# Down panels of the MLPs cut as 512, 272, 272 or 448, 448, 160 columns in place of three times 352

## What is computed

```python
hn = rmsnorm(x, p['norm_ffn_pre'][l])
f = jnp.square(jax.nn.relu(hn @ p['mlp_up'][l])) @ p['mlp_down'][l]
x = x + rmsnorm(f, p['norm_ffn_post'][l])
```

## Time and profile before

| | |
|---|---|
| time, two runs | 2158.47 and 2158.26 us, median 2158.36 |
| profiled execution, span from first to last instruction | 2155.1 us (its time with what lies around the span is not listed apart) |
| median of the runs less that span | 3.3 us |
| PE, PEld busy | 2146.0, 2135.0 us |
| DVE, ACT, POOL busy | 908.0, 652.9, 100.1 us |
| matmuls | 13496, of 352 columns but for the small products named above |
| the first of the four changed groups | its down units are evacuated from 591.30 to 679.02 us |

### The profile page before, as it was taken

How to read it: one execution, slowest core, us unless ns; L and a number is a source line. 1 busy time by engine, 2 the same in 40 slices (tenths; PEclk the granted TensorE clock), 3 DMA queues, 4 the chain that set the end, 5 groups by cost and what they waited for, 6 DMA issues and landing times.

```text
span 2155.1 us, 31488 instructions
## 1 busy us (share of the span) xinstructions
PE 2146.0 (100%) x13496; PEld 2135.0 (99%) x13496; DVE 908.0 (42%) x1414; ACT 652.9 (30%) x1105; POOL 100.1 (5%) x127
## 2 busy tenths in 40 slices
PE   9999999999999999999999999999999999999998
PEld 9999999999999999999999999999999999999998
DVE  8766367323322322334953333493223223322336
ACT  6673355202301310333511112453013103202332
POOL 2000000000000000000043231000000000000000
PEclk9999999999999999999999999999999999999999
DMA  5111422111111111141311114222111111111142
GB/s 165 35 41 40 139 88 72 50 40 49 50 42 47 49 50 40 49 135 44 120 50 47 43 50 139 67 84 59 42 48 50 49 40 50 50 42 48 50 140 81
DMA packets 208410, 138.65 MB, mean 64 GB/s; under 512 B 6000, under 2 KB 204784, under 8 KB 208272
## 3 DMA queue, kind: packets, MB, share of 16 engines
q1 hardware_dynamic: 207552, 135.51, 20.6%
q10 hardware_dynamic: 720, 1.13, 0.1%
HBM read 119.22 MB, written 17.40 MB: 63 GB/s over the span
## 4 chain that ended last, share of the span: by engine, by line
PE 99%; ACT 1%; DMA 0%; DVE 0%; issue 0%; DVEq 0%; ACTq 0%
PE ps L698 32%; PE ps L700 32%; PE ps L699 32%; PE ps L773 1%; PE ps L801 0%; PE ps L729 0%; PE ps L720 0%; DMA w_all_raw<-in_w_in_even_dram 0%; PE ps L716 0%; PE ps L784 0%; PE ps L760 0%; ACT L1074 0%; ACT L1030 0%; ACT lru L1030 0%; ACT lru L1032 0%; ACT gelu L1074 0%
## 5 line engine op out<-in xcount | busy, mean ns | idle before, releaser
L698 PE MATMUL ps<-x_hi,w_all 128*128 128x352 f32 x2304 | 747.0, 324 | 0.0
L700 PE MATMUL ps<-x_hi,w_all 128*128 128x352 f32 x2304 | 739.1, 321 | 0.0
L699 PE MATMUL ps<-x_lo,w_all 128*128 128x352 f32 x2304 | 739.1, 321 | 0.0
L698 PE MATMUL ps<-h_hi,w_all 128*128 128x352 f32 x1728 | 556.2, 322 | 0.0
L700 PE MATMUL ps<-h_hi,w_all 128*128 128x352 f32 x1728 | 555.2, 321 | 0.0
L699 PE MATMUL ps<-h_lo,w_all 128*128 128x352 f32 x1728 | 555.2, 321 | 0.0
L698 PEld LDWEIGHTS ps<-x_hi,w_all 128*128 128x128 f32 x2304 | 432.4, 188 | 2.7
L699 PEld LDWEIGHTS ps<-x_lo,w_all 128*128 128x128 f32 x2304 | 432.4, 188 | 2.2
L700 PEld LDWEIGHTS ps<-x_hi,w_all 128*128 128x128 f32 x2304 | 432.3, 188 | 0.0
L876 ACT CAST w_all<-w_all_raw 128x1024 fp32r<-128x1024 f32 x166 | 173.5, 1045 | 525.1 <-DMA w_all_raw<-in_mlp_down_dram 324.8
L698 PEld LDWEIGHTS ps<-h_hi,w_all 128*128 128x128 f32 x1728 | 324.5, 188 | 0.3 <-DVE h_lo L1452 0.3
(11 more groups left out here) (201 smaller groups left out, 1416.0 us busy)
## 6 DMA issues: line engine op xcount, KB each, us to landing
w_all_raw<-in_mlp_up_dram SPq DMA_DIRECT2D x60, 512.0 KB, 3.9
w_all_raw<-in_mlp_down_dram SPq DMA_DIRECT2D x60, 512.0 KB, 3.8
x_save<-f SPq DMA_DIRECT2D x9, 1408.0 KB, 6.0
x_old<-x_save SPq DMA_DIRECT2D x9, 1408.0 KB, 11.5
w_all_raw<-in_c_w_in_dram SPq DMA_DIRECT2D x22, 512.0 KB, 3.7
w_all_raw<-in_w_in_even_dram SPq DMA_DIRECT2D x12, 512.0 KB, 3.6
x_old<-in_x_cols_dram SPq DMA_DIRECT2D x3, 1408.0 KB, 12.8
w_all_raw<-in_w_out_even_dram SPq DMA_DIRECT2D x6, 512.0 KB, 3.8
```

Of the source, the lines that this page charges most:

```text
L698: nc.tensor.matmul(dst, wh, hi, start=(i == 0), stop=False)
L699: nc.tensor.matmul(dst, wh, lo, start=False, stop=False)
L700: last = nc.tensor.matmul(dst, wl, hi, start=False, stop=(i == KC - 1))
```

## The change

In the kinds `dn` with m other than 0 (4 groups of 7 panels, 28) the three units of a panel no longer take columns 0 to 352, 352 to 704 and 704 to 1056. With an odd m they take 512, 272 and 272, with an even m 448, 448 and 160. A table `columns` holds the bounds for each unit. PE reads h and VectorE updates f by that table (`cut`). The number of units, their order, their banks and all that surrounds them stay. The wait of an evacuation that adds to f is now for the last unit of the same panel number in the group before, since its pieces need not match. There are 12 panels with 160 columns and 16 with 272.

```diff
@@ -175,6 +175,9 @@
+    CUTS = ((0, 448, 896, TOK), (0, 512, 784, TOK))
+    columns = [(u.t * TT, (u.t + 1) * TT) if u.kind != "dn" or u.m == 0 else CUTS[u.m % 2][u.t:u.t + 2] for u in UNITS]
@@ -342,7 +345,11 @@
         def bank(n):
-            return ps[:, n % NB, 0:TT]
+            return ps[:, n % NB, 0:columns[n][1] - columns[n][0]]
+
+        def cut(buf, c, n):
+            c0 = c * (buf.shape[1] // KC)
+            return buf[:, c0 + columns[n][0]:c0 + columns[n][1]]
@@ -693,7 +700,7 @@
-                    hi, lo = pt(src[0], k, t), pt(src[1], k, t)
+                    hi, lo = [pt(b, k, t) if X else cut(b, k, n) for b in src]
@@ -1288,8 +1295,8 @@
                 if u.kind in ("dn", "dn3"):
-                    dve.wait_ge(evac_d, evac_no[n - 48] + 1)
-                    ins = nc.vector.tensor_tensor(pt(f, m, t), bank(n), pt(f, m, t), ALU.add)
+                    dve.wait_ge(evac_d, evac_no[n - 48 + NT - 1 - t] + 1)
+                    ins = nc.vector.tensor_tensor(cut(f, m, n), bank(n), cut(f, m, n), ALU.add)
```

## The result

The changed kernel takes **2192.7 us** (2192.46 to 2192.95, 2 runs) against 2158.36 (2158.26 to 2158.47, 2 runs): a ratio of 1.0159, 95% interval 1.0129 to 1.0188. It is 34.3 us slower where I forecast 10.2, and outside my range. The two profiled spans stand 35.4 us apart.

What follows compares the result with a forecast made beforehand. TensorE was taken as the bound: the number of matmuls times the distance at which they follow each other. The narrow piece's 10.2 us plus 0 for the rest, on 2158.4, gave 2168.6 us; range 2157 to 2180.

Steps and rivals of the forecast that it cites:

- Step 2: 160-column matmuls in even panels: each costs 35.5 ns more than a linear sum allows, x 288 = 10.2 us.
- floor: Least distance between matmuls that each bring a full set of weights: 0.111 us, hidden by 352 and 272 columns.
- the line: Linear cost of a matmul by its columns: 75.5 ns taken for 160, between 72.2 and 78.7.
- Step 1: Matmul count and columns in the cut panels: three pieces together cost the same, 476.7 ns; wider pieces cost nothing net.
- the 12 ns: Excess of a 352-column matmul's 158.9 ns over 146.7 at full clock, read as a fixed share or in proportion.
- Step 3: Where pieces begin: 3.84 or 3.80 us units differ in starting column; taken as zero, ends -1.0 and +1.9 us.
- Steps 4 to 6: VectorE's evacuations and subtractions, weight loads and casts, and the later down units' new wait: all covered, at no cost.
- A: Rival for the narrow matmuls: weight loads can follow closer than 0.111 us, so the change costs 0, 2158.4 us; 6%.
- B: Rival: narrow matmuls in the even panels fall to the full f32 rate, 267 ns each, 2213.6 us; 14%.
- C: Rival: half rate for the narrow piece, 145.3 ns each, 20.1 us more, 2178.5 us; 4%.
- D: Rival: the weight path sets 158.9 ns, so 272 and 160 columns cost that too; 36.9 us more, 2195.3 us; 5%.
- E: Rival: the granted clock drops in the thinner stretches, slower by over 2%; 1%.

Runs made afterwards that it cites:

- Experiment 9: The change with all 28 panels cut 512, 272, 272 and no narrower piece; 2162.13 us against 2157.79 for the kernel before, ratio 1.002.
- experiments 4 and 7: One extra 272-column matmul ahead of each of four up groups: in the kernel before (4), 2178.76 us against 2158.42; in the changed kernel (7), 2172.55 against 2157.79.
- experiment 8: The changed kernel with twelve other cuts in m = 1 to 6 and m = 7 back to 352 columns; 2177.39 us against 2158.76.

## Why the prediction was wrong

*Step 2, the narrow piece: right.* I said 111 ns for a floor and 75.5 for the line, 10.2 us. Measured: 111.7, and the line through 272 (125.1) and 512 (232.5) gives 75.0 at 160. 36.7 x 288 = 10.6 us. The row that carried it was the distance of two weight loads behind matmuls that take no time. The trace after has the loads of the narrow unit at the same distance:

```profile
621.92 0.19 PEld L706 LDWEIGHTS ps<-h_lo,w_all 128*128 128x128 f32 x1
622.03 0.19 PEld L707 LDWEIGHTS ps<-h_hi,w_all 128*128 128x128 f32 x1
622.14 0.19 PEld L705 LDWEIGHTS ps<-h_hi,w_all 128*128 128x128 f32 x1
```

*Step 1, "the three pieces together cost the same": mis-sized by 4 us.* 512, 272 and 272 columns take 232.5 + 2 x 125.1 = 482.7 ns, not 476.7. Neither reading of the 12 ns held: 272 fits the fixed share (125.3), 512 lies above both (225 and 231). The line through 272 and 512 passes 352 at 160.9 ns, but the kernel before runs it at 158.9. It sits 2 ns under the line, and each of 28 x 72 matmuls that leaves 352 gives that up: 4.0 us. Experiment 9, which has nothing but this term and no narrow piece, measures 4.3. I had the two readings of the 12 ns and no third in which 352 is a good width by itself.

*Step 3 is the step that failed.* "Where the pieces begin" saw that units of the same work take 3.80 or 3.84 us, and put the difference down to the starting column, a property of the unit. So I priced it inside the cut panels, at -1.0 to +1.9 us. The starting column does go with the 3.84: of the 80 units of the trace before that read the middle tile of h (columns 352 to 704), 75 take 3.84 us, and four of the other five hold column sums. But there is also a pace that the stream of matmuls on PE carries along, which a different sequence shifts and which then holds over unchanged work: 96 units at 4.00 instead of 3.80, 19.1 us (experiments 4 and 7). The sum had no term for a change of pace behind the cut panels.

No up group of the trace before shows 4.00 us, but an early stretch does, and I had not read it. Its unit from 42.88 us on, behind column sums, has all 24 matmuls 0.167 us apart at a granted clock of 1.00, and so has one from 30.62 us on:

```profile
42.88 0.33 PE L698 MATMUL ps<-x_hi,w_all 128*128 128x352 f32 x1
43.05 0.33 PE L699 MATMUL ps<-x_lo,w_all 128*128 128x352 f32 x1
43.22 0.33 PE L700 MATMUL ps<-x_hi,w_all 128*128 128x352 f32 x1
...
46.88 0.33 PE L698 MATMUL ps<-x_hi,w_all 128*128 128x352 f32 x1
```

VectorE was busy for 3.70 of these 4.00 us, so this stretch alone does not show why. Still, a rival "the units behind the cut panels run at 4.00 us" could have been priced from it: 96 x 0.2 = 19 us.

*Steps 4 to 6, VectorE, weights, waits at nothing: right.* The waits of PE after are two of the three short ones before.

*The rivals.* A, B and C fall with 111.7 ns for 160 columns. D would have given 2195.3, near the measured 2192.7 by luck, and is wrong in mechanism: 272 columns stand at 125.1 ns, not at 158.9. E did not happen in the change, where the clock stayed at full speed behind the 160-column units, but it did behind 32 columns.

10.6 + 4.0 + 19.1, and 0.5 + 0.5 for the slow first units of the changed and the unchanged down groups behind them, are 34.7 us. Measured were 34.3 in the times and 35.4 between the spans, which hold the 0.8 us of the early stretch.

What stays open is which property of the sequence sends the 352-column stream into the one pace or the other. The runs show that 272 columns flip it from either side, that 16 to 128 do not (from the quick pace; of these only 96 was tried from the slow one), that widths between can do either, and that the middle unit of a down panel, which starts at column 352 of its chunk, ends the slow pace, while up panels, with another spacing of their tiles, have no such unit. Whether the start addresses are the reason wasn't tried.

## What to carry to other kernels

Price a narrower matmul that brings its own 128 x 128 weights by max(weight-load distance, columns), and read the first from a place where tiny matmuls sit between full weight loads. Where PE is busy all the time, check whether equal units are equally spaced. Read the early stretches for this as well as the one that is changed. If there are two spacings, an edit can move a whole later stage from one to the other without touching it, so compare the pace of unchanged stages first. Such a shift can also be brought about, or undone, by a single extra matmul, and a small gain or loss of a tuned kernel should be checked for it before it is explained by the edit itself.

## What the hardware showed that I had not expected

- A stream of 352-column fp32r matmuls, each with its weight load, has at least two lasting paces, 158.3 and 166.7 ns, at the same full clock. One matmul of 272 columns ahead of it switched it in either direction (2158.4 to 2178.8 us, and 2192.7 to 2172.6).
- The same unit, with the same code ahead of it, ran at the quick pace in eight traces and at the slow one in three (it begins at 131.17 us in the trace before).
- From 32 to 192 columns such a matmul costs 111.5 to 111.8 ns. The Trainium skill ("TensorE: Matmul & The Clock Gate", section on LDWEIGHTS) has 107 ns for the load of 128 columns, 128 over 1.2 GHz; the measured distance is 5 ns more.
- Over the floor, the time beyond the columns at 2.4 GHz grows from 12 ns at 256 columns to 20 at 496. It is neither a fixed share nor a constant proportion.
- 24 matmuls of 32 columns in a row, with PE busy throughout by the profile, were followed by 3 us at a granted clock of 0.50, twice in one run (experiment 8).
